# Where the activation tiles start in SBUF: two start offsets replaced by eight lanes of 64 bytes

## What is computed

```python
def first_block(x, mem, ...):
    h = rms_norm(x, norm_mix_g)
    proj = h @ w_in + b_in                       # "x0": w1, px, py, gate1
    ...
    merged = sigmoid(...) * y_a + sigmoid(...) * y_b
    x = x + merged @ w_mix_out                   # "mix"
    x = x + cross_attention(...)                 # "c"
    x = x + conv_ffn(rms_norm(x, norm_ffn_g))    # "f"
    return rms_norm(x, norm_final_g)

def second_block(x, mem, ...):
    for l in range(2):
        x = x + 0.5 * rms_norm(swiglu(h, ffn1_w13[l], ffn1_w2[l]), ...)   # ("a", l)
        y = token_mixing(h, w_in[l], ...)                                 # ("m", l)
        x = x + rms_norm(y, ...)
        x = x + rms_norm(cross_attention(h, m, ...), ...)                 # ("c", l)
        x = x + 0.5 * rms_norm(swiglu(h, ffn2_w13[l], ffn2_w2[l]), ...)   # ("b", l)
    return x
```

## Time and profile before

| | |
|---|---|
| median of 3 runs (lowest to highest) | 2041.23 us (2040.38 to 2043.33) |
| the profiled execution, its own time | 2043.33 us |
| its span | 2041.2 us |
| TensorE matmuls busy | 2006.1 us, 98% of the span |
| VectorE, ScalarE, GpSimd busy | 66%, 53%, 2% |
| HBM read | 353.65 MB, 174 GB/s over the span |

### The profile page before, as it was taken

The page is one execution under the profiler, slowest core; times in us unless marked ns, Lnnn a source line. Parts: engine busy times, 40 slices in busy tenths (PEclk is TensorE's granted clock), DMA queues, the critical chain, the costliest instruction groups (busy, mean ns, idle before and its releaser), DMA issues.

```text
span 2041.2 us, 34241 instructions
## 1 busy us (share of the span) xinstructions
PE 2006.1 (98%) x13588; PEld 1786.8 (88%) x13588; DVE 1353.1 (66%) x1909; ACT 1089.8 (53%) x1739; POOL 49.9 (2%) x47
## 2 busy tenths in 40 slices
PE   8999999999999999999999999999999999999998
PEld 8989988999888889899988888888899999887887
DVE  6776766787566657866766555655477667656554
ACT  6846555555554454556556444644464555646443
POOL 0021000000000000000100000000000001000000
PEclk9999999999999999999999999999999999999999
DMA  7522454666565557534554655565565535445553
GB/s 279 166 75 78 153 169 163 205 206 196 166 215 190 186 165 237 183 130 130 196 197 134 224 181 194 184 202 187 191 202 187 176 114 176 162 163 182 185 186 124
DMA packets 98716, 359.08 MB, mean 176 GB/s; under 512 B 11192, under 2 KB 11512, under 8 KB 98296
## 3 DMA queue, kind: packets, MB, share of 16 engines
q1 hardware_dynamic: 98560, 356.90, 53.0%
HBM read 353.65 MB, written 1.05 MB: 174 GB/s over the span
## 4 chain that ended last, share of the span: by engine, by line
PE 91%; DVE 4%; ACT 3%; issue 1%; DMA 0%; DVEq 0%; SPq 0%; ACTq 0%
PE ps L998 10%; PE ps L1000 9%; PE ps L999 9%; PE ps L986 8%; PE ps L1176 8%; PE ps L1178 8%; PE ps L1177 8%; PE ps L1063 6%; PE ps L1065 6%; PE ps L1064 6%; PE ps L1032 2%; PE ps L1030 2%; PE ps L1031 2%; PE ps L1145 1%; DVE wlo L1668 1%; ACT whi L2400 1%
## 5 line engine op out<-in xcount | busy, mean ns | idle before, releaser
L1668 DVE TENSOR_TENSOR wlo<-raw,whi 128x1024 fp32r<-128x1024 f32 x635 | 773.5, 1227 | 404.4 <-ACT whi L2400 400.0
L2400 ACT ACTIVATE whi<-raw 128x1024 fp32r<-128x1024 f32 x635 | 666.2, 1057 | 402.4 <-PE ps L1065 152.1
L998 PE MATMUL ps<-H,whi 128*128 128x256 f32 x1328 | 379.4, 286 | 2.2 <-DVE wlo L1668 2.1
L999 PE MATMUL ps<-L,whi 128*128 128x256 f32 x1328 | 370.7, 279 | 0.0
L1000 PE MATMUL ps<-H,wlo 128*128 128x256 f32 x1328 | 370.7, 279 | 0.0
L1176 PE MATMUL ps<-whi,H 128*128 128x512 f32 x704 | 279.6, 397 | 4.0 <-DVE wlo L1668 2.1
L1178 PE MATMUL ps<-whi,L 128*128 128x512 f32 x704 | 275.2, 391 | 0.0
L1177 PE MATMUL ps<-wlo,H 128*128 128x512 f32 x704 | 274.8, 390 | 0.0
L998 PEld LDWEIGHTS ps<-H,whi 128*128 128x128 f32 x1328 | 250.8, 189 | 7.8 <-issue 4.2
L999 PEld LDWEIGHTS ps<-L,whi 128*128 128x128 f32 x1328 | 250.6, 189 | 0.6
L1000 PEld LDWEIGHTS ps<-H,wlo 128*128 128x128 f32 x1328 | 250.8, 189 | 0.0
(11 more groups left out here) (438 smaller groups left out, 3259.0 us busy)
## 6 DMA issues: line engine op xcount, KB each, us to landing
raw<-in_ws SPq DMA_DIRECT2D x635, 512.0 KB, 3.4
prow<-in_rows SPq DMA_DIRECT2D x11, 512.0 KB, 5.6
row<-in_rows SPq DMA_DIRECT2D x9, 512.0 KB, 6.3
mema<-in_memT SPq DMA_DIRECT2D x4, 512.0 KB, 4.7
mema<-in_mem2T SPq DMA_DIRECT2D x4, 512.0 KB, 5.9
memb<-in_mem2T SPq DMA_DIRECT2D x4, 512.0 KB, 5.3
DT<-in_dec SPq DMA_DIRECT2D x2, 768.0 KB, 6.4
X<-in_x SPq DMA_DIRECT2D x1, 1024.0 KB, 10.4
```

Of the source, the lines that this page charges most:

```text
L998: e.matmul(o, h, hs[k], start=first and k == 0, stop=False, skip_group_check=True)
L999: e.matmul(o, h, ls[k], start=False, stop=False, skip_group_check=True)
L1668: e.tensor_tensor(m.wlo[:, n % SPL, :], r, h.bitcast(F32), SUB).then_inc(*c.lo.done(n))
L2400: e.activation(m.whi[:, n % SPL, :], m.raw[:, n % RAW, :], ACT.Copy).then_inc(*c.hi.done(n))
```

## The change

The two start offsets are replaced by eight lanes. `H_store` and `L_store` become 8192 + 512 bytes, and a stage's H and L both start 64 x `LANE_OF[s]` bytes into them. `SLACK`, `SIDE`, `SPREAD`, `BEGIN` and `HIDDEN` go away: the temporary tensors stand at their plain distance from `low`, which itself lies 512 bytes further. HH and HL are plain tensors, and ("o", l) uses the start of "mix". No instruction, wait or order of steps is changed in the source.

```diff
-SLACK, SIDE = 256, 64
-SPREAD = (16, 40, 58, 82.5)
-BEGIN = {"x0": (64, 64), "mix": (0, 0), "c": (64, 64), "f": (64, 64), ("a", 0): (0, 0), ("m", 0): (64, 64), ("o", 0): (0, 0), ("c", 0): (64, 64), ("b", 0): (0, 0), ("a", 1): (0, 0), ("m", 1): (64, 64), ("o", 1): (0, 0), ("c", 1): (64, 64), ("b", 1): (0, 0)}
-HIDDEN = {"f": (0, 0), ("a", 0): (0, 0), ("b", 0): (0, 0), ("a", 1): (0, 0), ("b", 1): (0, 0)}
+LANE, LANES = 16, 8
+LANE_OF = {"x0": 1, "mix": 0, "c": 2, "f": 3, ("a", 0): 0, ("m", 0): 4, ("c", 0): 5, ("b", 0): 1, ("a", 1): 2, ("m", 1): 6,
+           ("c", 1): 7, ("b", 1): 4}
...
-        self.H_store = kept("H", [128, 8 * T + SLACK // 4], F32R)
-        self.L_store = kept("L", [128, 8 * T + SLACK // 4], F32R)
+        self.H_store = kept("H", [128, 8 * T + LANES * LANE], F32R)
+        self.L_store = kept("L", [128, 8 * T + LANES * LANE], F32R)
...
-        def at(name, kb, shape, dt=F32, lane=0):
-            kb += sum(SLACK for start in SPREAD if kb >= start) / 1024
-            off = low + (int(kb * 1024) + 63) // 64 * 64 + lane
+        def at(name, kb, shape, dt=F32):
+            off = low + (int(kb * 1024) + 63) // 64 * 64
...
-        self.HH_store, self.HL_store = (at(n, kb, [128, 22 * T + SLACK // 4], F32R) for n, kb in (("HH", 42.5), ("HL", 64.5)))
+        self.HH, self.HL = at("HH", 42.5, [128, 22, T], F32R), at("HL", 64.5, [128, 22, T], F32R)
...
-        self.YH, self.YL = two("YH", 62, 2, half, F32R, SIDE - SLACK), two("YL", 58, 2, half, F32R, SIDE - SLACK)
+        self.YH, self.YL = two("YH", 62, 2, half, F32R), two("YL", 58, 2, half, F32R)
...
-        self.BH, self.BL = at("BH", 110.25, four, F32R, SIDE), at("BL", 114.25, four, F32R, SIDE)
+        self.BH, self.BL = at("BH", 110.2, four, F32R), at("BL", 114.2, four, F32R)
...
-        self.QH, self.QL = at("QH", 8, [128, 3, T], F32R, SIDE), at("QL", 11, [128, 3, T], F32R, SIDE)
+        self.QH, self.QL = at("QH", 8, [128, 3, T], F32R), at("QL", 11, [128, 3, T], F32R)
...
-        self.BRH = [at(f"BRH{n}", kb, four, F32R, SIDE) for n, kb in enumerate((50.5, 8, 74.5))]
+        self.BRH = [at(f"BRH{n}", kb, four, F32R) for n, kb in enumerate((50.5, 8, 74.5))]
...
     def high(self, s):
 
-        return self.begun(self.H_store, 8, BEGIN[s][0])
+        return self.lane(self.H_store, LANE_OF[s])
...
+    def lane(self, store, n):
+        return store[:, LANE * n:LANE * n + 8 * T].rearrange("p (k t) -> p k t", k=8)
...
         if kind == "m":
-            return 8, "w_out_2", s[1], m.high(("o", s[1])), m.low(("o", s[1])), lambda k: dve.after("ml2", s[1], k // 2)
+            return 8, "w_out_2", s[1], m.high("mix"), m.low("mix"), lambda k: dve.after("ml2", s[1], k // 2)
```

More of the change, by code:

```diff
@@ L816, in at, with two @@
             return nc.alloc_sbuf_tensor_at(name, shape, dt, offset=off)
-        def two(name, kb, step, shape, dt=F32, lane=0):
-            return [at(f"{name}{i}", kb + step * i, shape, dt, lane) for i in range(2)]
+        def two(name, kb, step, shape, dt=F32):
+            return [at(f"{name}{i}", kb + step * i, shape, dt) for i in range(2)]
         full8, half, four = [128, 8, T], [128, 2, T], [128, 4, T]
         self.K, self.VV = at("K", 0, full8), at("VV", 8, [128, 2, 1024])
-        self.mems = [[at("mem" + x, kb, full8), at("mh" + x, kb2, full8, F32R, lane), at("ml" + x, kb2 + 8, full8, F32R, lane)]
-                     for x, kb, kb2, lane in (("a", 16, 24, SIDE), ("b", 98.6, 58.5, 0))]
+        self.mems = [[at("mem" + x, kb, full8), at("mh" + x, kb2, full8, F32R), at("ml" + x, kb2 + 8, full8, F32R)]
+                     for x, kb, kb2 in (("a", 16, 24), ("b", 98.6, 58.5))]
         self.smm, self.rbm = at("smm", 40, [128, T]), at("rbm", 41, [128, T])
@@ L848, in __init__ @@
         self.msk = at("msk", 53, [128, NMSK - 1024])
-        self.GG, self.BO, self.YA = two("GG", 58, 2, half, lane=SIDE - SLACK), two("BO", 62, 2, half, lane=SIDE - SLACK), two("YA", 66, 2, half)
-        self.YH, self.YL = two("YH", 62, 2, half, F32R, SIDE - SLACK), two("YL", 58, 2, half, F32R, SIDE - SLACK)
+        self.GG, self.BO, self.YA = two("GG", 58, 2, half), two("BO", 62, 2, half), two("YA", 66, 2, half)
+        self.YH, self.YL = two("YH", 62, 2, half, F32R), two("YL", 58, 2, half, F32R)
         self.PX, self.PY = at("PX", 70, [128, 4, T + 3]), at("PY", 74.1, four)
@@ L870, in __init__ @@
         self.swapped = {"rq": at("RS", 16, four), "qa": at("QS", 20, [128, 1, T]), "mq": at("MS", 24, full8), "dq": at("DS", 32, full8)}
-        self.QH, self.QL = at("QH", 8, [128, 3, T], F32R, SIDE), at("QL", 11, [128, 3, T], F32R, SIDE)
-        self.rbq, self.rbk = at("rbq", 14, [128, T], lane=SIDE), at("rbk", 15, [128, T], lane=SIDE)
+        self.QH, self.QL = at("QH", 8, [128, 3, T], F32R), at("QL", 11, [128, 3, T], F32R)
+        self.rbq, self.rbk = at("rbq", 14, [128, T]), at("rbk", 15, [128, T])
         self.GT = [[at(f"GT{n}{i}", 16 + 8 * n + 2 * i, half) for i in range(4)] for n in range(3)]
@@ L877, in __init__ @@
         self.E, self.EE, self.PT = two("E", 112, 2, [128, 2, 256]), two("EE", 42.5, 2, [128, 2, 256]), two("PT", 94.5, 2, [128, 2, 256])
-        self.BRH = [at(f"BRH{n}", kb, four, F32R, SIDE) for n, kb in enumerate((50.5, 8, 74.5))]
-        self.BRL = [at(f"BRL{n}", kb + 4, four, F32R, SIDE) for n, kb in enumerate((50.5, 8, 74.5))]
+        self.BRH = [at(f"BRH{n}", kb, four, F32R) for n, kb in enumerate((50.5, 8, 74.5))]
+        self.BRL = [at(f"BRL{n}", kb + 4, four, F32R) for n, kb in enumerate((50.5, 8, 74.5))]
         self.MG = at("MG", 82.5, full8)
@@ L887, in high @@
     def high(self, s):
-        return self.begun(self.H_store, 8, BEGIN[s][0])
+        return self.lane(self.H_store, LANE_OF[s])
     def low(self, s):
[L893 to L904, removed]
+        return self.lane(self.L_store, LANE_OF[s])
+    def lane(self, store, n):
+        return store[:, LANE * n:LANE * n + 8 * T].rearrange("p (k t) -> p k t", k=8)
     def mem(self, i):
@@ L1050, in outward @@
         name, layer = ("w_ffn_out", 0) if s == "f" else ({"a": "ffn1_w2_2", "b": "ffn2_w2_2"}[kind], s[1])
-        return 22, name, layer, m.hidden_high(s), m.hidden_low(s), lambda k: dve.after("hl", s, k // 2)
+        return 22, name, layer, m.HH, m.HL, lambda k: dve.after("hl", s, k // 2)
     def columns_of(s, name, layer, k, col):
@@ L2102, in fin_rest @@
         e.wait_ge(*act.after("hh", s, j))
-        tt(m.hidden_low(s)[:, 2 * j:2 * j + 2, :], m.UP[j % 2][:, :, :], m.hidden_high(s)[:, 2 * j:2 * j + 2, :].bitcast(F32), SUB, ("hl", s, j))
+        tt(m.HL[:, 2 * j:2 * j + 2, :], m.UP[j % 2][:, :, :], m.HH[:, 2 * j:2 * j + 2, :].bitcast(F32), SUB, ("hl", s, j))
     def fin_out(s, p):
@@ L2137, in hidden_turned @@
         e.wait_ge(*act.after("hh", s, g))
-        tt(m.hidden_low(s)[:, 2 * g:2 * g + 2, :], pair(banks.of("ht", s, g)), m.hidden_high(s)[:, 2 * g:2 * g + 2, :].bitcast(F32), SUB, ("hl", s, g))
+        tt(m.HL[:, 2 * g:2 * g + 2, :], pair(banks.of("ht", s, g)), m.HH[:, 2 * g:2 * g + 2, :].bitcast(F32), SUB, ("hl", s, g))
         banks.free(dve, "ht", s, g)
@@ L2365, in merged @@
         e.wait_ge(*act.after("mh2", l, i // 2))
-        stt(m.low(("o", l))[:, i:i + 2, :], m.MG[:, i:i + 2, :], 0.5, m.high(("o", l))[:, i:i + 2, :].bitcast(F32), MUL, SUB, ("ml2", l, i // 2))
+        stt(m.low("mix")[:, i:i + 2, :], m.MG[:, i:i + 2, :], 0.5, m.high("mix")[:, i:i + 2, :].bitcast(F32), MUL, SUB, ("ml2", l, i // 2))
     run = {"first": first, "mem": mem, "jy": jy, "jx": jx, "jn": jn, "jh": jh, "mem_rms": mem_rms, "keys_out": keys_out, "mem_cols": mem_cols,
@@ L2729, in fin_out @@
             e.wait_ge(*dve.after("up", s, j))
-            do(m.hidden_high(s)[:, 2 * j:2 * j + 2, :], m.UP[i][:, :, :], ACT.Copy, ("hh", s, j))
+            do(m.HH[:, 2 * j:2 * j + 2, :], m.UP[i][:, :, :], ACT.Copy, ("hh", s, j))
     def wide_out(s, g):
@@ L2740, in hidden_turned @@
         e.wait_ge(*pe.after("ht", s, g))
-        do(m.hidden_high(s)[:, 2 * g:2 * g + 2, :], pair(banks.of("ht", s, g)), ACT.Copy, ("hh", s, g))
+        do(m.HH[:, 2 * g:2 * g + 2, :], pair(banks.of("ht", s, g)), ACT.Copy, ("hh", s, g))
     def angles(p):
@@ L2872, in merged @@
         e.wait_ge(*dve.after("mg", l, 2, i))
-        do(m.high(("o", l))[:, i:i + 2, :], m.MG[:, i:i + 2, :], ACT.Copy, ("mh2", l, i // 2), scale=0.5)
+        do(m.high("mix")[:, i:i + 2, :], m.MG[:, i:i + 2, :], ACT.Copy, ("mh2", l, i // 2), scale=0.5)
     run = {"first": first, "mem": mem, "mem_rms": lambda i: root(("mem_rms", i), 1024),
```

## The result

The changed kernel takes 2055.04 us (median of 4 runs, 2053.24 to 2056.61), the kernel before 2041.03 us (2040.38 to 2043.33): +14.0 us, a ratio of 1.0066 with an interval of 1.0049 to 1.0084. It is slower, as forecast; 2053.3 had been predicted. The interval leaves no doubt of the direction, though the size is under 1%.

What follows compares the result with a forecast made beforehand. TensorE's matmul-to-matmul steps were taken as the bound; terms 2.8 + 2.8 - 1.3 + 7.8 = +12.1 us on the 2041.2 us median gave 2053.3 us. Forecast's own range 2047 to 2059, whole range 2037 to 2066.

Steps and rivals of the forecast that it cites:

- What bounds: Whole kernel: TensorE busy 2006.1 of 2041.2 us, so time is the sum of steps from one matmul to the next.
- Stationary H of the wide stages: Wide stages ("b", 0) to start 64 and ("a", 1) to 128: slower 512-column matmuls, +2.8 us each.
- Stationary 64 to 0: Values of memory 1 and mixer 0's rv and dv turn fast, -1.3 us; mixer 1's, at 128, taken as 0.
- Moving, off 64: 256-column matmuls whose moving start leaves 64: the 1,824 fast ones slow from 113.3 to 117.8 ns, +7.8 us.
- all slow at 117.8: Step assumed for every 256-column matmul whose moving start leaves 64; those already at 117.8 ns cost nothing more.
- a dearer pace: Rival: all 5,064 256-column matmuls leaving 64 step at 120.0 ns, +12.2 us over the forecast, 2065.5 us; chance 0.15.
- The moves by multiples of 256 and ("o", l): HH, HL, OH, OL and memory b move by multiples of 256, ("o", l) becomes "mix": no effect.
- The median against the profile: Profiled execution took 2043.33 us, slowest of three; the sum is added to the median, 2041.23 us.
- The signs: Durations expected: "f" 279 ns, wide stages 394, mixer 0's rv and dv 389, mixer 0 and BR unchanged at 279.
- The distance decides: Rival: moving minus stationary start modulo 256 sets the pace, only 192 bad; net -7.1 us, 2034.1 us; chance 0.12.
- No effect: Rival: what went before sets the pace, not the start; 2041.2 us, chance 0.13.

Runs made afterwards that it cites:

- the whole-shift run: Weights and all activations start 64 bytes further, distances unchanged, against the kernel before: 2042.92 us against 2042.58, ratio 1.0000.
- the run with the wide stages alone: Kernel before with only H and L of wide stages ("b", 0) and ("a", 1) starting at 64 and 128: 2046.81 us against 2042.58, ratio 1.0020.
- the experiments on start and distance: Kernel before with weights and all activations 64 bytes further: 2042.92 us; with whi and wlo alone 64 bytes further: 2065.02 us (one run); both against 2042.58.

## Why the prediction was right

1. **What bounds.** Right. Of the 17.3 us of span, 15.8 lie from one weight product's start to the next; 1.0 is a later first matmul and 0.6 the rest of TensorE's work. Counts and order are as before.
2. **Stationary H of the wide stages.** Right in place and nearly in size: +2.9 for ("b", 0) beside +2.8, and +2.4 where I had put +2.8 for the unshown start 128. Its step is 232.4 ns, 0.9 below the one at 64 that I took for it.
3. **Stationary 64 to 0.** Right: -1.2 found beside -1.3, and mixer 1's rv and dv at 128 gained 0.1, where I had 0.
4. **Moving, off 64.** The mechanism was right, and this is the term that was mis-sized: +7.8 predicted, +13.7 found in the profiled execution. A small part is in its own working: the two rows differ by (4.71 - 4.53)/40 = 4.5 ns, not 4.3, which makes the term 8.2. The step "all slow at 117.8" holds at 192 alone ("f", +4.7). The matmuls that were slow already were put at nothing, and those that went to 0 took another 2.2 ns each: BR, Q, B and Y cost 1.9 us. At 0 the step is 120.0 ns, at 128 some 119 on average, single steps from 115 to 123. The figure of 120.0 had been my upper bound, and the rival *a dearer pace* gave it to all 5,064 matmuls: it holds for the 2,568 at 0, nearly for the 1,248 at 128, and not for the 1,248 at 192. The whole lies between the forecast and this rival.
5. **The moves by multiples of 256 and ("o", l).** Nothing, as predicted: HH and the output products kept 226.7 to 227.0 ns. (The prediction's "some 3,800" matmuls of the 512 form are 4,500 in the trace; no sum uses the figure.)
6. **The median against the profile.** The stages of the two profiled executions say +17.3, the medians +14.0. A part of this is that a distance of 64 can take either step, so that the kernel before is not the same in each execution: the profile before has "f" at 113.4 throughout, the whole-shift run has it at 117.9 with the same distances, and in the run with the wide stages alone three of the key batches had 117.8 that had 113.3 before, at an unchanged distance. "f" alone is worth 4.7 us, and the kernel before ranged over 5.3 us in 19 runs (2040.18 to 2045.43). That it is "f" which varied in those timed runs is argued, since they have no profile.
7. **The signs.** The wide stages at 394 and 395 ns and rv and dv at 389 came as named. Two signs failed. Mixer 0 and BR were to stay at 279 ns and have 283. And "f" has 281, which by the prediction's "280 or more" would have been the dearer pace, while its step is 117.8, the forecast's own.

That 2055.0 came so close to 2053.3 is in part luck. The whole moving term was priced from two steps at one start, and three new starts then had a price each; a gap of 5.9 us in that term shrank to 1.7 in the median, mostly because the two profiled executions lie 3.3 us further apart than the medians.

**The rivals.** *The distance decides* named the right quantity (the experiments on start and distance) and had the wrong sign: I carried the order of the 512 form (0 good, 192 bad) over to the 256 form, and there 0 is the worst of the four and 192 is better than 0 and 128. *No effect* is refuted by the ratio of 1.0066. By the Trainium skill's rule on two independent read ports ("TensorE: Matmul & The Clock Gate", "Part 2: What happens when you issue a matmul") the time would have stayed the same. This trace doesn't agree for fp32r operands: the same matmul with the same load beside it steps by 113.3 to 120.0 ns, by the distance of the two addresses.

**What stays open.** Why these distances and no others. The runs show a function of the distance that repeats after 256 bytes and depends on the form; they don't show what collides. Nor do they show what decides between 113.3 and 117.8 ns at 64, only that at 112 the short step comes back. And most distances were seen in one profiled execution of one stage; where a distance has two steps, one such reading can miss the other.

## What to carry to other kernels

Where TensorE is the bound, look at the steps from matmul to matmul by stage: two steps for one shape at one granted clock, without a wait between, are a reason to look at where the operands lie. Then what is to be chosen is the distance between the moving and the stationary tile, for each form by itself, and it costs one probe with another start in each stage to read a dozen of them. Take a start that finds the short step again after a disturbance, rather than one that merely has it in the profile at hand.

## What had not been expected of the hardware

- The step of an fp32r matmul of 256 columns depends on the distance of its operands modulo 256 bytes: 120.0 ns at 0, 113.3 or 117.8 at 64, 113.3 at 112, 120.1 at 104, 117.8 at 192. With 512 columns: 226.7 at 0 and at 136 (rv and dv at 120), 228.9 at 64, 232.4 at 128, 233.3 at 192; at 240 (start 16) 226.7 in HH, and 226.7 or 233.3 in a wide stage.
- Two steps can be stable at one distance (64), and the one that is taken may hold for a thousand matmuls: "f" had 113.3 ns for 1,056 of them in one run and 117.8 in another.
- Eight bytes are worth up to 7.0 us of 127 in one stage ("f" at 104 beside 112).
